# The causal mask matmul moved ahead of the rotary products, and the last rotary product cut to 64 rows

## The reference

```python
q_pe = apply_rope(rms_norm(q[..., QK_NOPE:], g_q_rope), cos, sin)      # 64 channels per head
k_pe = apply_rope(rms_norm(k_rope, g_k_rope)[:, :, None, :], cos, sin) # one key for all heads
k = jnp.concatenate([k_nope, jnp.broadcast_to(k_pe, (B, S, H, QK_ROPE))], axis=-1)
qh = jnp.concatenate([q_nope, q_pe], axis=-1) * (QK_DIM ** -0.5)
s = jnp.einsum('bhqd,bhkd->bhqk', q_i, kh).astype(jnp.float32)         # 128 + 64 channels
s = jnp.where(kpos[None, :] <= qpos[:, None], s, NEG_INF)              # causal
prob = jax.nn.softmax(s, axis=-1).astype(vh.dtype)
return jnp.einsum('bhqk,bhkd->bhqd', prob, vh)
```

## Time and profile before

| | us |
|---|---|
| median of 3 runs | 1186.24 (1185.19 to 1186.58) |
| the profiled execution | 1186.24 |
| its span | 1184.5 |
| TensorE busy | 1123.7 (95%) |
| VectorE busy | 845.2 (71%) |
| ScalarE busy | 776.1 (66%) |
| GpSimd busy | 397.9 (34%) |
| mean granted TensorE clock | 0.994 |

### The profile page before, as it was taken

One profiled execution on the slowest core, in us unless ns is written; L12 is line 12 of the kernel. 1 busy time (PEld: TensorE's weight loads), 2 busy tenths in 40 slices (PEclk: granted clock), 3 DMA queues, 4 the chain that ended last, 5 costly groups with the idle time before them and its releaser, 6 DMA issues. The chain is left out here.

```text
span 1184.5 us, 17694 instructions
## 1 busy us (share of the span) xinstructions
PE 1123.7 (95%) x5403; PEld 909.3 (77%) x5403; DVE 845.2 (71%) x1208; ACT 776.1 (66%) x1274; POOL 397.9 (34%) x475
## 2 busy tenths in 40 slices
PE   5999999999899999899999999999999999999898
PEld 5988888788677764788888887777777887777576
DVE  6335524177664445999999998898898989888573
ACT  5634424257553222889898887788788888888471
POOL 1110000033373001355555554444454554544200
PEclk9999999999999999999999999999999999999899
DMA  6322312112303078699999999999999999999611
GB/s 235 131 83 71 142 71 72 39 58 85 111 2 124 36 315 329 245 334 366 383 389 388 386 387 387 360 354 366 365 356 374 372 369 368 380 364 337 206 49 54
DMA packets 71805, 291.52 MB, mean 246 GB/s; under 512 B 15123, under 2 KB 20278, under 8 KB 46806
## 3 DMA queue, kind: packets, MB, share of 16 engines
q1 hardware_dynamic: 52422, 254.15, 55.1%
q0 software_dynamic: 18768, 34.79, 11.5%
q10 hardware_dynamic: 576, 2.10, 0.4%
HBM read 284.61 MB, written 42.07 MB: 276 GB/s over the span
## 5 line engine op out<-in xcount | busy, mean ns | idle before, releaser
L1411 DVE TENSOR_TENSOR arena_r<-arena,win_r 128x1024 fp32r<-128x1024 f32 x252 | 292.0, 1221 | 57.8 <-ACT win_r L943 54.0
L943 ACT ACTIVATE win_r<-arena 128x1024 fp32r<-128x1024 f32 x252 | 246.2, 1056 | 56.0 <-DMA arena<-in_w_exp_up 54.9
L1786 PE MATMUL bank<-win_r,work_r 128*128 128x512 f32 x512 | 205.4, 401 | 18.7 <-DVE x_low_r L1392 16.1
L664 POOL DMA_INDIRECT moe_sum<-ya,sidx x64 | 116.5, 1820 | 255.0 <-ACT ya L972 248.4
L1787 PE MATMUL bank<-win_r,x_low_r 128*128 128x512 f32 x512 | 199.4, 390 | 0.0
L1788 PE MATMUL bank<-arena_r,work_r 128*128 128x512 f32 x504 | 197.1, 391 | 0.0
L1431 DVE TENSOR_TENSOR arena_r<-arena,hT_r 128x1024 fp32r<-128x1024 f32 x128 | 150.5, 1217 | 0.0
L1786 PEld LDWEIGHTS bank<-win_r,work_r 128*128 128x128 f32 x512 | 96.3, 188 | 41.8 <-issue 21.2
L1553 PE MATMUL bank<-arena_r,hT_r 128*128 128x512 f32 (+2 forms) x320 | 120.9, 378 | 0.0
L1554 PE MATMUL bank<-arena_r 128*128 128x512 f32 (+2 forms) x320 | 120.7, 377 | 0.0
L1557 PE MATMUL bank<-win_r,hT_r 128*128 128x512 f32 (+2 forms) x320 | 120.6, 377 | 0.0
(11 more groups left out here) (273 smaller groups left out, 2152.1 us busy)
## 6 DMA issues: line engine op xcount, KB each, us to landing
arena<-in_w_exp_down SPq DMA_DIRECT2D x64, 1024.0 KB, 15.5
arena<-in_w_exp_gate SPq DMA_DIRECT2D x63, 1024.0 KB
arena<-in_w_exp_up SPq DMA_DIRECT2D x63, 1024.0 KB
win<-in_w_in SPq DMA_DIRECT2D x8, 2048.0 KB, 7.7
win<-in_w_o SPq DMA_DIRECT2D x2, 2048.0 KB, 7.6
arena<-in_w_ple_gate SPq DMA_DIRECT2D x2, 2048.0 KB, 21.4
arena<-moe_sum SPq DMA_DIRECT2D x8, 512.0 KB, 8.5
win<-in_mla_w_qb SPq DMA_DIRECT2D x4, 576.0 KB, 4.0
```

The lines of the kernel that those rows point to most:

```text
L664: pool.indirect_dma_start(sums[j % 2], bass.IndirectOffsetOnAxis(sidx[j % 2][0:NS, 0:1], 0), yo[j % 2][0:NS], None, bounds_check=last_toke ...
L943: act.activation(gu_hi[n % 2][:, :, cols], raw[:, :, cols], ACT.Copy).then_inc(gu_hi_r, 1)
L1411: dve.tensor_tensor(low_[:, :, cols], raw[:, :, cols], gu_hi[n % 2][:, :, cols].bitcast(F32), ALU.subtract).then_inc(gu_lo_r, 1)
L1786: pe.matmul(b_, x_hi[:, k, :], w_hi, start=(k == 0), stop=False)
```

## The change

In each of the 32 score steps the mask product now comes directly behind the product without rotation, ahead of the wait for `rope_lo` and of both rotary products. The product against `kpe_lo` takes only the 64 rows that hold the high part of the query (rows 0 to 63 for even heads, 64 to 127 for odd ones), ends the group and raises `s_done`. The low times low term is no longer added. The columns (W) of all products are as before.

```diff
                 if s < NA:
                     h, i = divmod(s, NT)
-                    W = (i + 1) * P
+                    W, r0 = (i + 1) * P, ROPE * (h % 2)
                     if s >= 2:
                         pe.wait_ge(exp_done, s - 1)
                     b_ = bank[s % 2]
                     pe.matmul(b_[:, 0:W], qT[:, h, tok(i)], kT[:, h, 0:W], start=True, stop=False)
+
+                    pe.matmul(b_[:, i * P:W], identb[:, :], negmask[:, :], start=False, stop=False)
                     if i == 0:
                         pe.wait_ge(rope_lo, h + 1)
                     pe.matmul(b_[:, 0:W], q_st[:, h % 2, tok(i)], kpe_hi[:, 0:W], start=False, stop=False)
-                    pe.matmul(b_[:, 0:W], q_st[:, h % 2, tok(i)], kpe_lo[:, 0:W], start=False, stop=False)
-                    pe.matmul(b_[:, i * P:W], identb[:, :], negmask[:, :], start=False, stop=True).then_inc(s_done, 1)
+                    pe.matmul(b_[:, 0:W], q_st[r0:r0 + ROPE, h % 2, tok(i)], kpe_lo[r0:r0 + ROPE, 0:W],
+                              start=False, stop=True).then_inc(s_done, 1)
```

## The result

| | before | after |
|---|---|---|
| median of 5 runs | 1186.58 us (1185.19 to 1187.82) | 1194.22 us (1191.57 to 1196.79) |
| ratio | | 1.0065, 95% interval 1.0047 to 1.0083 |
| span of the profiled execution | 1184.5 us | 1194.8 us |
| attention loop, first score product to the first transpose behind it | 67.2 us | 74.2 us |

The change makes the kernel slower by 0.65%, 7.7 us (5.6 to 9.8 by the interval). The forecast was 1193.7. One execution of a kernel in the experiments (mask last, 64 rows) took 5725.5 us and is left out of its ratio.

A forecast was written before the change was run, and what follows sets the result against it. TensorE was taken to bound the loop, GpSimd next. Height changes, 10.0 us after a 0.9 deduction, less 2.5 slack, plus 0 for mask and rows, gave +7.5 on 1186.24: 1193.7 us, range 1185.0 to 1203.0.

The forecast's parts named there:

- That TensorE bounds the loop, and what follows carries it on: Attention loop: TensorE busy 15.73 of 16 us, so loop losses or gains carry 1:1 to the end.
- The mask product, moved, at nothing: 32 score steps: moving the mask product ahead costs 0, between -0.5 and +0.4 us.
- 0.07 us, wherever it stands: Score stream: the mask product's slot costs 0.07 us in any place, so no gain from its place.
- Fewer rows save nothing: Low product: halving rows leaves its stream at about 0.23 us with 512 columns; shorter loads save 0.2 us at most, taken as 0.
- The price of a change of height: Around the 64-row product: 64 changes between full and half height at 0.17 us each, 10.9 us.
- a pace of 0.11 and a tail of 0.06: Each height change: load exposed in full, 0.11 us, plus 0.06 us of the preceding product's tail.
- The slack of 2.5 us: Transposes' waits for the exponential, 3.9 us in all, shrink as TensorE arrives later; 2.9 available, 2.5 us taken off.
- 0.9 us for the 128-column entries: Eight entries in 128-column steps, where loads already set the pace: 8 x 0.11 = 0.9 us taken off.
- A free change of height: Rival at the 64-row product: height changes cost nothing, loads use the spare store; 1186.2 us, chance 0.33.
- the rival that the change does nothing: Whole change: instruction count and columns stay, no work saved; falls together with the free height change, no chance of its own.
- Full serialization: Rival: each height change waits for the product ahead to finish, then loads; +17.3 us, 1203.5 us, chance 0.10.
- Faster: Rival at each score step's exit: free rows let loads start sooner, saving 3.5 us, 1182.7 us; chance 0.10.

The follow-up runs named there:

- mask first: Kernel before with only the mask product moved ahead of both rotary products, low product kept at 128 rows: ratio 1.0030, again 1.0018 against the kernel before.
- the doubled kernels: Low product issued twice in a row, in the kernel before (128 rows, ratio 1.0033) and in the change (64 rows, 1.0123), both against the kernel before.

## Why the prediction was right

**That TensorE bounds the loop, and what follows carries it on**: right. +7.0 us in the loop, and 108.2 us to the experts' part in both.

**The mask product, moved, at nothing**: wrong, and outside its bounds (-0.5 to +0.4 us). It costs 0.04 us in each of 32 steps, 1.3 us, 0.8 of it in the loop's length. The step that failed is "0.07 us, wherever it stands": that slot was read with the transposes behind the mask. What I left out is the load of the rotary operand that now stands there, with a pace of 0.11 us; both orders with the mask ahead of a rotary product cost 0.04 to 0.05 us a step.

**Fewer rows save nothing**: right. 183 ns per load against 190, and the second product of each pair streams alike.

**The price of a change of height**: right in its mechanism, and in its size for the two changes of a step together. The prediction took 0.17 us for each. Over mask first the change costs 0.34 us in each of the three widths without a wait (1.23 - 0.89, 1.67 - 1.33, 2.10 - 1.76), 0.17 per change in the mean. The two are not alike. By the ends (start + duration, and durations of matmuls are modelled) in the rows of a 256-column step above, the low product ends 0.12 us behind the first rotary product with 128 rows (344.85 - 344.73) and 0.32 with 32 (341.09 - 340.77): +0.20. The transpose ends 0.11 us behind it (344.96 - 344.85) against 0.26 (341.35 - 341.09): +0.15. The low product's own load is recorded with 183 ns, and the transposes' with 140. With the bf16 mask behind the low product the price is 0.28 for both. What differs is the load behind. The two, by their forms in the kernel after:

```profile
L1640 PEld LDWEIGHTS bank<-ident,arena 128*128 128x128 f32 x63 | 6.7, 140 | 4.7 <-issue 2.8 <-ACT arena L841 1.0
...
L1628 PEld LDWEIGHTS bank<-negmask,identb 128*128 128x128 bf16 x25 | 2.5, 98 | 2.5 <-issue 1.4
```

140 ns recorded for the transposes', 98 for the mask's. That the price falls with a shorter load is what one expects if the load is exposed; the 105 ns on the low product's duration are part of the same exposure on the way in. So 0.20, 0.15 and, for the mask, some 0.08 (0.28 less 0.20) go along with the recorded lengths of the loads, 180, 140 and 98 ns. The prediction made up its 0.17 otherwise, of a pace of 0.11 and a tail of 0.06 that no run shows by itself; that the mean came out the same is partly luck. The Trainium skill's rule that changing the tiling mode drains TensorE (TensorEngine Tiling, Key Properties) agrees with loads that no longer start ahead at a change, and with a price of 0.34 us for a pair of changes; the rows don't show the drain itself. Its list of configurations (Available Configurations: 128, 64 or 32 rows) agrees with 96 rows being free. The rule on loads (TensorE: Matmul & The Clock Gate, LDWEIGHTS: columns count, rows don't) is closer to the trace, 183 against 190 ns, than the 35-row load had suggested.

**The slack of 2.5 us**: right in place, low in size. 32 x 0.34 = 10.9, plus 1.3 for the mask, is 12.2, and 7.0 arrived: some 5 us were taken in. I counted it from the waits that the profile labels (3.9 us), and took off 0.9 us for the 128-column entries, which the runs don't separate from slack. The labelled waits fell by only 2.1 us, to 1.8, so they don't hold all the slack, and "the only slack in the loop" was wrong of them. From start to start, the 512-column steps of the second to seventh head took in 1.6 us (1.94 to 2.06 us before, with a wait, against 1.73 without; 2.10 to 2.12 after), and the 128-column steps behind the first head 2.9, if the price is the same there. Two errors of about 1.5 us, the mask and the slack, went opposite ways. That the sum of 7.5 comes so near to the 7.0 of the loop is luck: it is better than its terms.

**The rivals.** A free change of height falls with the 64-row and the doubled kernels, and with it the rival that the change does nothing. Full serialization at 0.33 us a change falls: 0.17 in the mean, 0.20 at most. Faster falls: every step is longer, and the loads around the 64-row product start later and not sooner.

## What to carry to other kernels

Cutting the rows of a matmul did not make it cheaper: beside a neighbour of its own height, a 64-row product took as much of the stream as a 128-row one (0.24 and 0.23 us with 512 columns). A product of 64 rows or fewer in a stream of full-height ones pays for both changes of height, here 0.34 us a pair (measured at 64 and at 32 rows); if such products are needed, put them side by side, or fill the operand up to full height as the kernel before does. And where a short product is moved in an order, price the load behind it, not only its own stream.

## What was not expected of the hardware

- The price is for the height's class and not for the rows: 96 rows cost nothing, 64 and 32 rows the same 0.34 us per step (steps of 0.90, 1.23 and 1.23 us with 256 columns).
- A bf16 product of 128 columns seems not to cover the load of a float32 operand behind it: 0.04 to 0.05 us per step in both places ahead of a rotary product. That the load is the cause is the reading that fits, and was not tested apart.
- The part of 700 us behind the attention differs by over 4 us between two executions of the same program (708.4 and 713.0 us), while the loop repeats to 0.15 us. The length of the stage that was edited tells more than the total.
